# Modulation of c by row products summed on VectorE over a transposed w_ada

## The reference, cut to what matters

```python
for l in range(DEPTH):                       # DEPTH = 2
    mod_l = (silu(c)     @ w_ada[l] + b_ada[l]).reshape(b_, 1, N_MOD, D_MODEL)   # N_MOD = 9
    mod_c = (silu(c_ctx) @ w_ada[l] + b_ada[l]).reshape(N_MOD, D_MODEL)
    # sublayer j uses rows 3j, 3j+1, 3j+2 as shift, scale, gate
    h = rmsnorm(x, nw) * (1 + scale) + shift
    x = x + FFN_RES * gate * rmsnorm(swiglu(h, w_in_ff, w_out_ff), nw_post)
```

## Time and profile before

| | |
|---|---|
| time, median of 3 | 2924.2 us |
| the profiled execution: span | 2921.0 us |
| TensorE matmul busy | 2750.3 us (94%) |
| VectorE busy | 1458.4 us (50%) |
| ScalarE busy | 869.2 us (30%) |
| DMA, mean over the span | 108 GB/s, 315.81 MB |
| mean granted TensorE clock | 0.974 of full |

### The profile page before, as it was taken

The page is one execution under the profiler, slowest core; times in us unless marked ns, Lnnn a source line. Parts: engine busy times, 40 slices in busy tenths (PEclk is TensorE's granted clock), DMA queues, the critical chain, the costliest instruction groups (busy, mean ns, idle before and its releaser), DMA issues.

```text
span 2921.0 us, 35967 instructions
## 1 busy us (share of the span) xinstructions
PE 2750.3 (94%) x14448; PEld 2459.3 (84%) x14448; DVE 1458.4 (50%) x1967; ACT 869.2 (30%) x1152; POOL 80.2 (3%) x40
## 2 busy tenths in 40 slices
PE   5999998998988989999999999999998988799998
PEld 2999997887966789999988899999887756688887
DVE  2555556655444665555465555554464555532233
ACT  3211112443422351111235511112353423522232
POOL 0000000100000110000001000000000000100001
PEclk9999999999989999999999999999999999799999
DMA  5333333332200233333343333333332301322231
GB/s 213 123 115 122 130 133 136 140 129 77 94 0 1 73 116 115 115 122 124 121 171 125 130 115 120 123 131 116 129 115 91 108 1 44 115 101 100 87 129 72
DMA packets 100973, 315.81 MB, mean 108 GB/s; under 512 B 6928, under 2 KB 23312, under 8 KB 87312
## 3 DMA queue, kind: packets, MB, share of 16 engines
q1 hardware_dynamic: 93744, 297.20, 29.3%
q10 hardware_dynamic: 7136, 17.30, 1.7%
HBM read 312.38 MB, written 2.10 MB: 108 GB/s over the span
## 4 chain that ended last, share of the span: by engine, by line
PE 87%; DVE 7%; ACT 2%; issue 2%; DMA 1%; POOL 0%; SPq 0%; POOLq 0%; DVEq 0%; ACTq 0%
PE ps L1529 46%; PE ps L1543 23%; PE ps L795 5%; PE ps L902 2%; PE ps L1572 2%; DVE w_lo L1266 2%; PE ps L1601 1%; PE ps L1611 1%; PE ps L885 1%; ACT w_hi L1059 1%; PE ps L876 1%; DVE acc L1292 1%; PE ps L938 1%; PE ps L1585 1%; PE ps L895 1%
## 5 line engine op out<-in xcount | busy, mean ns | idle before, releaser
L1529 PE MATMUL ps<-xn_hi,w_hi 128*128 128x384 f32 (+2 forms) x2528 | 725.2, 342 | 21.8 <-DVE arena L1351 16.9
L1529 PE MATMUL ps<-xn_lo,w_hi 128*128 128x384 f32 (+2 forms) x2528 | 721.6, 340 | 0.0
L1529 PE MATMUL ps<-xn_hi,w_lo 128*128 128x384 f32 (+2 forms) x2528 | 721.4, 340 | 0.0
L1266 DVE TENSOR_TENSOR w_lo<-raw,w_hi 128x2048 fp32r<-128x2048 f32 x211 | 499.6, 2368 | 375.7 <-ACT w_hi L1059 375.4
L1529 PEld LDWEIGHTS ps<-xn_hi,w_hi 128*128 128x128 f32 x2528 | 464.3, 189 | 33.9 <-issue 17.3
L1059 ACT ACTIVATE w_hi<-raw 128x2048 fp32r<-128x2048 f32 x211 | 400.5, 1898 | 283.7 <-PE ps L1543 225.8
L1529 PEld LDWEIGHTS ps<-xn_lo,w_hi 128*128 128x128 f32 x2528 | 465.5, 189 | 11.3
L1529 PEld LDWEIGHTS ps<-xn_hi,w_lo 128*128 128x128 f32 x2528 | 465.4, 189 | 11.0
L1162 ACT ACTIVATE arena<-ps 128x384 f32 (+3 forms) x158 | 72.8, 496 | 1102.8 <-PE ps L1529 1102.7
L1292 DVE SCALAR_TENSOR_TENSOR acc<-raw_ada,silu_c,acc 128x512 f32<-128x512 f32 x512 | 345.5, 746 | 4.5 <-DVE acc L1280 3.2
L1543 PE MATMUL ps<-w_hi,hj_hi 128*128 128x512 f32 x952 | 301.2, 398 | 17.7 <-DVE w_lo L1266 8.2
(11 more groups left out here) (183 smaller groups left out, 2288.5 us busy)
## 6 DMA issues: line engine op xcount, KB each, us to landing
raw<-w_ff_in SPq DMA_DIRECT2D x104, 1024.0 KB, 5.3
raw<-w_ff_out SPq DMA_DIRECT2D x77, 1024.0 KB, 4.8
raw_ada<-w_ada SPq DMA_DIRECT2D x128, 512.0 KB, 3.7
raw<-w_out SPq DMA_DIRECT2D x16, 1024.0 KB, 4.8
raw<-w_in SPq DMA_DIRECT2D x12, 1024.0 KB, 5.2
arena<-w_ada SPq DMA_DIRECT2D x4, 2048.0 KB, 17.5
gate_row<-norm_w ACTq DMA_DIRECT2D x12, 512.0 KB, 4.2
arena<-dft_l_in ACTq DMA_DIRECT2D x2, 2048.0 KB, 7.9
```

The source lines that it names most:

```text
L1266: nc.vector.tensor_tensor(w_lo[par][:, 0:width], raw[par][:, 0:width], w_hi[par][:, 0:width].bitcast(F32), ALU.subtract).then_inc(S["w_lo" ...
L1529: ins = mm(ps[:, 4 * b + part + c, col:col + wd], w[:, k, c, :], xx[:, k, t0:t0 + wd], start=(k == 0 and i == 0), stop=(k == KC - 1 and i ...
```

## The change: what it does

`w_ada` is passed transposed and cut into blocks of 128 columns: block (h, u) is 128 x 1024 float32 with the 128 output columns on the partitions and the 1024 inputs along each row. The vectors silu(c) and silu(c_ctx) are held as rows of 1024 on all partitions (`silu_row`, 128 x 2 x 1024). A unit is now one block: one load of 512 KB into `acc`, and for each vector one VectorE instruction over 128 x 1024, which multiplies the block with the row and writes the sum along the row into a column of `ada_col`. The product itself goes to a bfloat16 tile that nobody reads. The small matmuls and TensorE's waits for them go. For the halves of layer 1 from 10 on, which only the latent tokens use, only one vector is treated (`streams`).

There is one buffer for the blocks, `acc`, so a unit's load waits until the unit before it is done. In the in slots SyncE issues the load of the next slot ahead of the two units of a step; in the out slots its order stays as it was. `silu_row` is loaded and passed through Silu by ScalarE in the lead of the first sublayer. The first 4 halves are made as before, from a contiguous copy of their columns.

```diff
-ADA_IN = {(0, 0): [(0, 4, 9)], (0, 2): [(0, 16, 2), (1, 0, 7)], (1, 0): [(1, 9, 9)]}
+ADA_IN = {(0, 0): [(0, 4, 9)], (0, 2): [(0, 16, 2), (1, 0, 7)], (1, 0): [(1, 9, 1), (1, 10, 8)]}
+def streams(l, h):
+    return 1 if l == DEPTH - 1 and h >= 10 else 2
-        raw_ada = [sb(f"raw_ada{i}", [P, 2, HB]) for i in range(2)]
         acc = sb("acc", [P, 2, HB])
+        junk = sb("junk", [P, D], BF16)
+        silu_row = sb("silu_row", [P, 2, D])
+        ada_col = sb("ada_col", [P, 4, 2])
 # SyncE
-            def unit(count, l, col, u):
-                if not isinstance(count, int) or count >= 2:
-                    sp.wait_ge(S["ada_used"], count - 1 + START)
-                src = w_ada[l].rearrange("(u c p) n -> u p c n", c=2, p=P)[u, :, :, bass.ds(col, HB)]
-                sp.dma_start(raw_ada[u % 2][:], src).then_inc(S[f"ada_raw{u % 2}"], 16)
+            def unit(count, l, h, u):
+                sp.wait_ge(S["ada_used"], 2 * count + START)
+                src = w_ada_t[l].rearrange("(h u) p k -> u p h k", u=4)[u, :, bass.ds(h, 1), :].rearrange("p h k -> p (h k)")
+                sp.dma_start(acc[:].rearrange("p a n -> p (a n)"), src).then_inc(S["ada_raw"], 16)
-                    for k, n, f, s, half, _ in in_steps(sub, loop, (0, 0)):
-                        load(n, (par0 + s) % 2, w_ff_in[l, j // 2, f])
-                        if half is not None: ... unit, unit
+                    load(n0 + LEAD, (par0 + LEAD) % 2, w_ff_in[l, j // 2, LEAD])
+                    for k in ahead:                      # range(LEAD, FC + LEAD)
+                        if k + 1 in ahead:
+                            load(n0 + k + 1, (par0 + k + 1) % 2, w_ff_in[l, j // 2, (k + 1) % FC])
+                        if k in due:                     # the same steps as before
+                            hl, h = due[k]
+                            for u in (2 * (k % 2), 2 * (k % 2) + 1):
+                                unit(4 * (hl * HALVES + h) - 16 + u, hl, h, u)
 # ScalarE, called in the lead of the first sublayer between gate_silu of slot 1 and split_w of slot 3
+            def modulation_rows():
+                act.dma_start(silu_row[:], c_row_in.to_broadcast([P, 2, D])).then_inc(S["c_row"], 16)
+                act.wait_ge(S["c_row"], 16)
+                nc.scalar.activation(silu_row[:], silu_row[:], ACT.Silu).then_inc(S["silu_row"], 1)
 # VectorE
-            def unit(count, u): ... memset, then 4 scalar_tensor_tensor of 128x512 into acc
+            def unit(half, count, u, n_streams):
+                if u == 0:
+                    dve.wait_ge(S["fin_read"], half)
+                dve.wait_ge(S["ada_raw"], count * 16 + 16)
+                for s in range(n_streams):
+                    dve.wait_ge(S["ada_used"], count * 2 + (s + START))
+                    ins = nc.vector.scalar_tensor_tensor(out=junk[:], in0=acc[:].rearrange("p a n -> p (a n)"), scalar=1.0,
+                                                         in1=silu_row[:, s, :], op0=ALU.mult, op1=ALU.mult,
+                                                         accum_out=ada_col[:, u, s:s + 1])
+                    ins.then_inc(S["ada_used"], 2 // n_streams)
+            def finish_units(h, hl, units):              # after the fourth unit of a half
+                dve.wait_ge(S["ada_used"], units * 2 + START)
+                add_bias(h, hl, ada_col[:])
 # TensorE: finish_col (8 products of acc with ones) and its calls are removed, and so are the
 # waits on fin_read in project_in and before the out slots
```

More of the change, by code:

```diff
@@ L162, in tiles_of, with build @@
     return [list(range(first)), list(range(first, sum(sub["groups"])))]
-def build(nc, x_in, w_ada, norm_w, w_ff_in, w_ff_out, w_in, w_gates, w_out, w_qkv, cvec_in, gate_b_in,
+def streams(l, h):
+    return 1 if l == DEPTH - 1 and h >= 10 else 2
+def build(nc, x_in, w_ada0, w_ada_t, c_row_in, norm_w, w_ff_in, w_ff_out, w_in, w_gates, w_out, w_qkv, cvec_in, gate_b_in,
           b_col_in, nw_col_in, convw_in, convb_in, hn_w_in, fmix_in, dft_l_in, dft_c_in, dft_g_in, tri_in, out):
@@ L311, in build @@
             "w_raw0 w_raw1 w_hi w_lo w_used "
-            "ada_raw0 ada_raw1 ada_used fin_mm fin_read row_mm row_read silu_c "
+            "ada_raw ada_used c_row silu_row fin_mm fin_read row_mm row_read silu_c "
             "silu h_done hj_hi hj_lo "
@@ L348, in in_steps @@
                 yield k, n0 + k, k - FC, k % 2, half, (1,)
[L350 to L353, removed]
         def out_steps(sub, g, loop, per):
@@ L998, in _ @@
                             load(n0 + k, (par0 + k) % 2, w_ff_in[l, j // 2, k])
-                    for k, n, f, s, half, _ in in_steps(sub, loop, (0, 0)):
-                        load(n, (par0 + s) % 2, w_ff_in[l, j // 2, f])
[L1001 to L1004, removed]
+                    ahead = range(LEAD, FC + LEAD)
+                    halves = [(hl, h0 + i) for hl, h0, count in sub["ada_in"] for i in range(count)]
+                    due = {LEAD + 2 * i + s: half for i, half in enumerate(halves) for s in range(2)}
+                    if sub["ada_tail"]:
+                        due |= {FC + s: sub["ada_tail"] for s in range(2)}
+                    load(n0 + LEAD, (par0 + LEAD) % 2, w_ff_in[l, j // 2, LEAD])
[6 more added lines that the diff above has]
+                                unit(4 * (hl * HALVES + h) - 16 + u, hl, h, u)
                     w = w_ff_out[l, j // 2].rearrange("(s c p) n -> s p c n", c=2, p=P)
@@ L1021, in _ @@
                             hl, h, g0 = half
-                            unit(4 * g0 - 16 + u, hl, h * HB, u)
+                            unit(4 * g0 - 16 + u, hl, h, u)
             for p_ in range(NTL):
@@ L1198, in lead @@
                 gate_silu(sub, 1, n0 + 1, 1, 1, (0,))
+                if not prev:
+                    modulation_rows()
                 split_w(n0 + 3, 1 - par0)
@@ L1274, in hj @@
                 nc.vector.tensor_tensor(lo[:, 0:w], hidden(sub, g, c), hi[:, 0:w].bitcast(F32), ALU.subtract).then_inc(S["hj_lo"], 1)
-            def unit(count, u):
+            def unit(half, count, u, n_streams):
                 if u == 0:
[L1280 to L1297, removed]
@@ L1299, in finish_col, with add_bias @@
+            def add_bias(h, hl, src):
+                bias = b_col[:, bass.ds(h * 4, 4)].unsqueeze(2).to_broadcast([P, 4, 2])
+                dst = vecs[:, bass.ds(hl, 1), :, :].rearrange("p a c s -> p (a c) s")
+                nc.vector.tensor_tensor(dst, src, bias, ALU.add).then_inc(S["fin_read"], 1)
+            def finish_units(h, hl, units):
+                dve.wait_ge(S["ada_used"], units * 2 + START)
+                add_bias(h, hl, ada_col[:])
             def finish_col(h, hl, bank_):
@@ L1302, in finish_col @@
                 dve.wait_ge(S["fin_mm"], h + 1)
[L1303 to L1306, removed]
+                add_bias(h, hl, ps[:, bank_, GW:GW + 8].rearrange("p (c s) -> p c s", s=2))
@@ L1454, in _ @@
                         gate_half(sub, 1, 6)
-                    for k, n, f, s, half, groups in in_steps(sub, own.loop, (13, 0)):
+                    if not prev:
+                        dve.wait_ge(S["silu_row"], 1)
+                    for k, n, f, s, half, groups in in_steps(sub, own.loop, (0, 0)):
                         split_w(n + 1, (par0 + s + 1) % 2)
@@ L1459, in _ @@
                             for u in (2 * s, 2 * s + 1):
-                                unit(i * 4 + (4 * g0 - 16 + u), u)
+                                unit(i + g0, i * 4 + (4 * g0 - 16 + u), u, streams(hl, h0))
                             if s == 1:
-                                finish_col(i + g0, i + h0, 3)
+                                finish_units(i + g0, i + h0, i * 4 + (4 * g0 - 12))
                         if groups == (1,) and k == FC + LEAD - 1 and not sub["final"]:
@@ L1490, in _ @@
                         if half is not None:
-                            unit(4 * half[2] - 16 + u, u)
+                            unit(half[2], 4 * half[2] - 16 + u, u, streams(half[0], half[1]))
                             if u == 3:
-                                finish_col(half[2], half[1], 6)
+                                finish_units(half[2], half[1], 4 * half[2] - 12)
                         if st is not None:
@@ L1515, in _, with project_in @@
             pe.sem_inc(S["w_used"], START)
-            def project_in(sub, n, par, b, groups=(0, 1), taken=None):
+            def project_in(sub, n, par, b, groups=(0, 1)):
                 pe.wait_ge(S["w_lo"], n + 1 + START)
@@ L1522, in project_in @@
                 for c in range(2):
-                    if c == 1 and taken is not None:
-                        pe.wait_ge(S["fin_read"], taken)
                     for k in range(KC):
@@ L1565, in project_out @@
                     ins.then_inc(S["w_used"], 1)
[L1567 to L1574, removed]
             def gate_half(sub, i, b0):
@@ L1664, in _ @@
```

(3 more changed lines are left out.)

9 lines of the change are left out of this document (5 added, 4 removed).

## The result

The changed kernel takes 2937.05 us, the median of 4 runs (2936.09 to 2938.93), against 2924.14 us before beside it: a ratio of 1.0048, with a 95% interval of 1.0037 to 1.0060. It is slower by some 13 us. The span of the profiled execution is 2936.0 us, 15.0 above that of before.

A forecast was written before the change was run, and what follows sets the result against it. The prediction took TensorE, on 87% of the chain, to bound the kernel, with unit chains through SyncE, DMA, ScalarE and VectorE in some stretches. Its terms summed to +22.6 us, giving 2947 us, range 2918 to 2975.

The forecast's parts named there:

- loops, 27 halves: In-slot loops: TensorE loses 1.68 us of small matmuls a half, with VectorE keeping up; -45.4 us.
- last in slots of (0,0): Last in slots of the first sublayer: less TensorE waiting at small matmuls, part given back for lower clock; -7.2 us.
- out slots 0 to 8 of (0,0), (0,2): First 8 out slots of two sublayers: unit, load, split and next unit close in one step; +34.7 and +34.3 us.
- clock behind the phases: Slot after each out phase: TensorE restarts at a lower clock, 1.5 us a phase; +3.0 us, bounds 0 and 9.
- silu_row: Lead of the first sublayer: ScalarE's row load and Silu delay slot 3; +3.2 us, bounds 1.9 and 5.6.
- The step: Out slots with units: one turn of unit, load behind it, split, next unit; 14.05 us against TensorE's 8.20.
- The bounds given: Out step length: 12.55 us with landing 4.8 and unit 2.6; 15.25 with landing 7.0 and unit 3.1.
- a second wait in the loops: Loops: another wait ending where the small matmuls' did, so removing them frees nothing; excluded, no size or chance given.
- Rival 1: VectorE units: summing instruction at half rate, unit 5.0 us instead of 2.9; 3031 us, chance 0.10.
- Rival 2: Out slots: block hardly delays the load behind it, sum free, step 12.55 us; 2919 us, chance 0.20.
- break-even: Out step length at which the change would cost nothing, all else as in the sum: 12.45 us.
- Rival 3: Out phases: TensorE stays at the lower clock and bounds them at 16.4 us a slot; 2980 us, chance 0.05.

The follow-up runs named there:

- the pair of runs on the old method: Kernel before without its small matmuls, 2884.4 us; the same with loads one slot ahead in in and out slots, 2844.9 us.

## Why the prediction was right, point by point

The forecast was slower, 2947 us in 2918 to 2975; 2937.05 came. The direction and the mechanism of the loss hold. The sum gave +22.6 us against the profiled execution, whose span grew by 15.0. That makes 7.6 of the 10 us between forecast and result; another 2.1 are the step from span to median, for which 3.2 us were added and which is 1.05 in the changed kernel. By its terms:

| term | predicted | measured from the two traces |
|---|---|---|
| loops, 27 halves | -45.4 | 365.6 to 349.5 in (0,2) and in (1,0); three times -16.1 = -48.3 |
| last in slots of (0,0) | -7.2 | 41.3 (452.95 - 101.12 - 310.51) - 49.2 = -7.9 |
| out slots 0 to 8 of (0,0), (0,2) | +34.7, +34.3 | 105.2 - 75.7 = +29.5, 104.8 - 76.1 = +28.7 |
| clock behind the phases | +3.0 | 27.41 - 24.66 and 26.42 - 24.66: +4.5 |
| silu_row | +3.2 | +7.7: slots 2 to 21 of (0,0) 8.4 us shorter, less the loops' 16.1 |

Together +14.2 of the 15.0 us of the spans. That the total came so near is in part luck: the phases were put 11 us too long, and against that the lead 4.5 and the clock 1.5 us too short.

**Out phases.** This term was mis-sized most, by 11 us. The step was put at 14.05 us and is 13.27. (The terms as listed add up to 14.4; the 14.05 counts the 0.37 of the issue within the 0.45.) The sum's output costs 0.08 us an instruction, not 0.157 (below), the instruction 1.22, not 1.284, so a unit is 2.5 us; and the load behind a block lands in 5.70 to 5.87, not 6.0, in (0,0). Seven steps at 0.78 are 5.5 us a phase. The bounds given (12.55 and 15.25) held it.

**Loops.** The number was nearly right: 9 finishes of 1.68 us are 15.1 of the 16.1 us a sublayer, and the matmuls around them take 0.1 us a trip less than before as well. So was the working of the changed kernel's own cover: VectorE waits for the second block and is done in time. But one sentence was not: that a second wait in the loops "is excluded as far as the rows go: the chain is TensorE without a gap". The chain that ended last says nothing about how close the next one is. The kernel before, less its small matmuls, fell into one through SyncE's queue that took 34.4 us a trip in (0,0) and 36.3 in (1,0), against TensorE's 33.3. That the change escaped it because it moved the loads is argued from the pair of runs on the old method; I had read this move only as a part without price.

**silu_row.** The load took 7.01 us, not 5.5; the gap ahead of slot 3 was 4.9 us; and the slots behind it started at the lower clock, which I had priced only for the out phases. Slots 3 to 21 took 310.51 us where full clock gives 307.9, so 4.9 + 2.6 make up 7.5 of the 7.7. The run with the load issued earlier takes 7.6 us off slots 2 to 21.

**Rival 1**, half rate of the summing instruction, falls: it takes 1.22 us for 1024 elements, no more than the 1.284 of the same operation without a sum. The rule of the Trainium skill's "Vector Engine (DVE) Microarchitecture Reference", section "Points that are easy to get wrong", that such an operation with two sources that are not bfloat16 runs at half throughput, does not hold for this instruction with two float32 sources in SBUF, a multiplication in both places and a bfloat16 result; the measurement decides. The sentence of the Trainium skill's "VectorE: DVE Perf Modes", section "Two Vector instructions with no wait between them", that such an operation is two instructions, agrees with the trace, which shows a read of the accumulator behind every one (duration in ns min/median/max, first and last start):

```profile
L1300 DVE SCALAR_TENSOR_TENSOR junk<-acc,silu_row x224: 1212/1224/1228, 116.8 to 1998.4; 128x1024 bf16<-128x1024 f32 x112
L1300 DVE DVE_READ_ACCUMULATOR junk<-acc,silu_row x224: 79/81/85, 117.9 to 1999.6; 128x1 f32 x112
```

**Clock.** The prediction let a slower slot hide in its step and priced only the slot behind a phase. Both hold. In the stretch of one step (columns as above) TensorE is busy 10.07 us for work of 8.20 and idle for the rest, some 3.1 us.

```profile
489.50:502.70 13.20, 10.07 (x36) 7.82 (x36) 5.53 (x8) 2.67 (x4) 0.00 (x0) 0.87 0.33 119
```

Under a step of 13.27 that costs nothing; only the slots 8 to 10 pay, with 2.8 and 1.8 us where 1.5 each had been put.

**Rival 2** had the right direction of error: the step was shorter than I took, but 13.27 is above its break-even of 12.45. **Rival 3**, the lower clock throughout, did not come: the phases were granted 0.90.

## What to carry to other kernels

When a buffer is dropped, don't ask only whether its own load is still hidden; ask what stands behind that load in the same queue, and write down the loop unit -> wait -> next load -> unit with its length against the slot's. Here moving one load ahead of the waiting one turned +0.5% into -2.5%, and did the same for the old method in part. A chain that shows one engine without a gap says that this engine is the limit there now, not how much is gained by giving it less work: before counting on a removed piece, work out the period of the next loop of waits. And leave a margin for it, since the landing times in it can change with the change (5.5 to 6.7 us here).

## What the runs showed of the hardware

The block loads of 128 rows of 4 KB land in 3.3 us in the median, those of 256 rows of 2 KB in 3.7. The broadcast of 8 KB to 128 partitions (1 MB) takes 7.0 us, while the 1 MB loads of w_ff_out have a median of 4.9. The same 1 MB loads of w_ff_in in the loops of (1,0) land in 5.5 us in the median in the kernel before and in 6.7 without the small matmuls; the cause is open. In an out step of the changed kernel TensorE is idle for some 3.1 us, and its slot takes 10.1 instead of 8.20 us, with a granted clock of 0.87 of 2.4 GHz on average over the step. The summing instruction over two float32 sources of 128 x 1024 in SBUF takes 1.22 us, and the read of its accumulator 0.08.
